# Modulation units of a two-layer diffusion trunk: fp32 weight-stationary matmuls on unsplit weights, at other places in the order

## The reference

```python
mod = silu(c) @ w_mod[layer] + b_mod[layer]   # 6 * 1024 columns, for c and for c_ctx
shift1, scale1, gate1, shift2, scale2, gate2 = split(mod, 6)
h = modulate(rmsnorm(x, g), shift1, scale1)   # h * (1 + scale) + shift
x = x + gate1 * rmsnorm(mixer(h), g)
h = modulate(rmsnorm(x, g), shift2, scale2)
x = x + gate2 * rmsnorm(ffn_or_moe(h), g)
```

## Time and profile before

| | us |
|---|---|
| three runs | 2237.32, 2241.19 (median), 2241.66 |
| span of the profiled execution | 2240.4 |
| PE busy in it | 2015.4 (90%) |
| DVE busy | 1433.3 (64%) |
| ACT busy | 1210.4 (54%) |
| data read from HBM | 471.27 MB, 211 GB/s |

### The profile page before, as it was taken

How to read it: one execution, slowest core, us unless ns; L and a number is a source line. 1 busy time by engine, 2 the same in 40 slices (tenths; PEclk the granted TensorE clock), 3 DMA queues, 4 the chain that set the end, 5 groups by cost and what they waited for, 6 DMA issues and landing times.

```text
span 2240.4 us, 25373 instructions
## 1 busy us (share of the span) xinstructions
PE 2015.4 (90%) x9386; PEld 1603.1 (72%) x9386; DVE 1433.3 (64%) x1355; ACT 1210.4 (54%) x1227; POOL 68.4 (3%) x124
## 2 busy tenths in 40 slices
PE   4699778699999977878979999999999999999996
PEld 3587546488887846853768878788787878878785
DVE  3545473633323336455458888888888888888885
ACT  3644353433322236433537767676777777776773
POOL 0011000000000000113000000000000000000000
PEclk9899889899999988986959999999999999999998
DMA  8455202143332214521028989899998989899891
GB/s 277 149 170 174 72 1 75 38 151 125 122 112 94 94 38 146 190 81 31 22 94 330 365 308 368 307 362 336 348 361 307 367 313 364 323 353 361 314 364 51
DMA packets 266582, 473.49 MB, mean 211 GB/s; under 512 B 19416, under 2 KB 119056, under 8 KB 266512
## 3 DMA queue, kind: packets, MB, share of 16 engines
q1 hardware_dynamic: 262928, 469.33, 59.5%
q0 software_dynamic: 3456, 3.19, 0.6%
q10 hardware_dynamic: 128, 0.03, 0.0%
HBM read 471.27 MB, written 1.05 MB: 211 GB/s over the span
## 4 chain that ended last, share of the span: by engine, by line
PE 79%; DVE 11%; ACT 5%; issue 3%; DMA 1%; ACTq 0%; SPq 0%; DVEq 0%; POOL 0%
PE bank L478 22%; PE bank L479 22%; PE bank L480 22%; PE bank L527 2%; PE bank L646 2%; DVE split_low L462 2%; ACT split_high L457 2%; PE bank L347 2%; DVE overlay L371 2%; PE bank L1657 2%; DVE split_low L1421 2%; ACT overlay L406 1%; PE bank L621 1%; PE bank L1699 1%; PE bank L636 1%
## 5 line engine op out<-in xcount | busy, mean ns | idle before, releaser
L1421 DVE TENSOR_TENSOR split_low<-raw_weights,split_high 128x2048 fp32r<-128x2048 f32 x224 | 511.7, 2287 | 59.8 <-ACT split_high L1115 58.8
L1115 ACT ACTIVATE split_high<-raw_weights 128x2048 fp32r<-128x2048 f32 x224 | 429.3, 1920 | 147.7 <-PE bank L480 147.7
L462 DVE TENSOR_TENSOR split_low<-raw_weights,split_high 128x1024 fp32r<-128x1024 f32 x214 | 256.9, 1224 | 372.2 <-ACT split_high L457 372.1
L478 PE MATMUL bank<-h_high,split_high 128*128 128x512 f32 (+1 forms) x848 | 329.3, 388 | 47.6 <-DVE h_low L392 30.5
L457 ACT ACTIVATE split_high<-raw_weights 128x1024 fp32r<-128x1024 f32 x214 | 219.5, 1051 | 227.9 <-PE bank L480 210.8
L479 PE MATMUL bank<-h_low,split_high 128*128 128x512 f32 (+1 forms) x848 | 322.8, 381 | 0.0
L480 PE MATMUL bank<-h_high,split_low 128*128 128x512 f32 (+1 forms) x848 | 322.7, 381 | 0.0
L1421 DVE TENSOR_TENSOR h_low<-raw_weights,h_high 128x2048 fp32r<-128x2048 f32 x112 | 256.7, 2292 | 78.7 <-ACT h_high L1115 78.6
L478 PE MATMUL bank<-split_high,xe_high 128*128 128x512 f32 x672 | 272.2, 405 | 14.0 <-DVE split_low L1421 14.0
L479 PE MATMUL bank<-split_low,xe_high 128*128 128x512 f32 x672 | 267.6, 398 | 0.0
L480 PE MATMUL bank<-split_high,xe_low 128*128 128x512 f32 x672 | 265.2, 395 | 0.0
(11 more groups left out here) (242 smaller groups left out, 3028.9 us busy)
## 6 DMA issues: line engine op xcount, KB each, us to landing
raw_weights<-in_moe_w SPq DMA_DIRECT2D x336, 1024.0 KB, 6.6
raw_weights<-in_w_mod SPq DMA_DIRECT2D x48, 1024.0 KB, 5.3
raw_weights<-in_ffn_w SPq DMA_DIRECT2D x33, 1024.0 KB, 5.2
raw_weights<-in_ev_w_in SPq DMA_DIRECT2D x10, 1024.0 KB, 5.8
raw_weights<-in_od_w_in SPq DMA_DIRECT2D x8, 1024.0 KB, 5.6
raw_weights<-in_ev_w_out SPq DMA_DIRECT2D x4, 1024.0 KB, 5.5
raw_weights<-in_od_w_out SPq DMA_DIRECT2D x4, 1024.0 KB, 5.3
overlay<-in_rpb SPq DMA_DIRECT2D x32, 64.0 KB, 2.3
```

The source lines that it names most:

```text
L462: dve.tensor_tensor(half_of(s, j, SPL[:, s % NSPLIT, :]), half_of(s, j, raw_of(split_at[s])), half_of(s, j, SPH[:, s % NSPLIT, :]).bitcast ...
L478: pe.matmul(ps, wh, xh, start=first, stop=False)
L1115: act.activation(esplit(u)[0], RAW[:, u % NRAW, :], ACT.Copy).then_inc(S("e_high"), 1)
L1421: dve.tensor_tensor(lo, RAW[:, u % NRAW, :], hi.bitcast(F32), ALU.subtract)\
```

## The change

A modulation unit is no longer split. `pe_mods` makes the raw weights stationary, 16 tiles of 128x128 in fp32, and streams the two vectors (two columns), so that the result lies across partitions at once; `dve_mods` adds the bias straight out of the bank. The halves of the vectors, the row copies, the small DMAs and the summing matmuls go. A unit's buffer is released by the matmuls and not by its split.

The units leave `ev`, `up` and `od`. Of the 48, numbers 0 to 7 stay in the start; 8 to 15 go into the first attention, two ahead of every second P.V product; 16 to 23 go between the heads' norm sums and `evo`; 24 to 27 behind n1's sums, 28 to 31 behind n2's; 32 to 35 behind n3's, 36 to 39 behind n4's; 40 to 43 behind ckv's sums, ahead of the latent products; 44 to 47 between n5's sums and n6's. The loads follow that order, and SP's bias loads for the second attention now stand ahead of those of units 44 to 47. The splits for `evo` and `odo` are no longer made ahead of the attentions: `to` is held at the last unit of `ev` and `od`.

```diff
@@ weight_units
-    units += mods(0, 0, 8)
-    for s in range(10):
-        units.append(("split", "ev", cols(w["ev_w_in"][0], 256 * s)))
-        units += mods(0, 8 + 2 * s, min(10 + 2 * s, 24))
-    units += [("split", "evo", cols(w["ev_w_out"][0], 256 * s)) for s in range(4)]
+    units += mods(0, 8)
+    units += [("split", "ev", cols(w["ev_w_in"][0], 256 * s)) for s in range(10)]
+    units += mods(8, 18)
+    for s in range(4):
+        units.append(("split", "evo", cols(w["ev_w_out"][0], 256 * s)))
+        if s == 1:
+            units += mods(18, 24)
+    units += mods(24, 28)
...
-        units += mods(1, s, min(s + 1, 8))
+        if s == 0:
+            units += mods(28, 32)
...
+    units += mods(32, 36)
...
-        units += mods(1, 8 + 2 * s, 10 + 2 * s)
+        if s == 1:
+            units += mods(36, 40)
+    units += mods(40, 44)
...
+    units += mods(44, 48)
@@ dve_modulate
             tmp(0)
             tmp(1)
+            if first:
+                first(0, 0)
@@ in place of pe_mod, act_mod, move_rows, pe_mod_third, dve_mod_third
+        def pe_mods(pe, i0, i1, bank, base=0):
+            for i in range(i0, i1):
+                r = mod_at[i]
+                pe.wait_ge(S(f"raw{r % NRAW}"), need[r])
+                wt = raw_of(r).rearrange("p (k n) -> p k n", k=KT)
+                c0 = base + 4 * (i % 24)
+                for m in range(2):
+                    for k in range(KT):
+                        last = pe.matmul(PS[bank][:, c0 + 2 * m:c0 + 2 * m + 2], wt[:, k, P * m:P * m + P],
+                                         SC[:, k, :], start=(k == 0), stop=(k == KT - 1))
+                last.then_inc(S("mod_used"), 1)
+
+        def dve_mods(dve, v0, v1, bank, base=0):
+
+            l, m0, c0, n = v0 // 6, 8 * (v0 % 6), base + 16 * (v0 % 6), v1 - v0
+            dve.wait_ge(S("mod_used"), 4 * v1)
+            dve.tensor_tensor(MOD[:, l, m0:m0 + 8 * n, :],
+                              PS[bank][:, c0:c0 + 16 * n].rearrange("p (m v) -> p m v", v=2),
...
+            dve.wait_ge(S("mod_evac"), v1)
@@ pe_attention
                     if p >= 2:
                         pe.wait_ge(S(f"o_evac{a}"), p - 1)
+                    if p % 2 == 0 and p // 2 < len(mods):
+                        pe_mods(pe, *mods[p // 2], OBANK[0], 256)
                     for kt in range(u["nk"]):
@@ SP
             for r in range(len(UNITS)):
+                if r == mod_at[44]:
+                    load_bias()
@@ ACT
-            to(0)
...
             act_root(act, N["n0"])
+            to(0, 0)
             act.wait_ge(S("affine"), 1)
...
             for g, s in run("ev"):
-                to(g + 1)
+                to(min(g + 1, of["ev"][-1]))
@@ DVE
+            to(of["evo"][1])
+            dve_mods(dve, 2, 6, 5, 256)
...
             to(of["evo"][-1] + 1)
@@ PE
-                pe_mod(pe, f)
+                pe_mods(pe, f, f + 1, 7)
...
-            pe_attention(pe, 0, att0)
+            pe_attention(pe, 0, att0, [(8 + 2 * p, 10 + 2 * p) for p in range(4)])
             for h in range(4):
                 pe_sums(pe, N[f"sub{h}"])
+            pe_mods(pe, 16, 24, 5, 256)
...
             pe_sum_pair(pe, N["n1"], 3)
+            pe_mods(pe, 24, 28, 7)
             pe.wait_ge(*norm_root("n1"))
             pe_sums(pe, N["n2"])
+            pe_mods(pe, 28, 32, 7)
...
             pe_sums(pe, N["n3"])
+            pe_mods(pe, 32, 36, 7)
             pe.wait_ge(*norm_root("n3"))
             pe_sums(pe, N["n4"])
+            pe_mods(pe, 36, 40, 7)
...
             pe_sums(pe, N["ckv"])
+            pe_mods(pe, 40, 44, 2)
             pe.wait_ge(*norm_root("ckv"))
...
             pe_sum_pair(pe, N["n5"], 3)
+            pe_mods(pe, 44, 48, 7)
             pe.wait_ge(*norm_root("n5"))
             pe_sums(pe, N["n6"])
```

More of the change, by code:

```diff
@@ L238, in trunk @@
                 of.setdefault(stage, []).append(ns)
-                full_after.append((full_after[-1] if ns else 0)
-                                  + (0 if stage == "down" else 1 if stage[:3] == "mod" else 2))
+                full_after.append((full_after[-1] if ns else 0) + (0 if stage == "down" else 2))
                 ns += 1
@@ L250, in trunk @@
                 release.append(("direct_used", nd))
-        stage_of = [UNITS[r][1] for r in split_at]
         def run(stage):
[L257 to L263, removed]
+            return [(s, i) for i, s in enumerate(of[stage])]
         token_major = [of["ev"][i] for i in (2, 3, 8, 9)] + [of["od"][i] for i in (4, 5)]
-        mod_index = {s: i for i, s in enumerate(of["mod0"] + of["mod1"])}
         def raw_of(r):
@@ L375, in mod_vectors, with dve_modulate @@
             return VEC[:, l, 2 * which], MOD[:, l, 24 * which:24 * which + 8]
-        def dve_modulate(dve, n, c0, full=False):
+        def dve_modulate(dve, n, c0, full=False, first=None):
             nt, wd = n["nt"], n["width"]
@@ L448, in half_free @@
                 return unit_used(old)
-            return bank_full(old, j) if stage_of[old][:3] != "mod" else unit_used(old)
+            return bank_full(old, j)
         def act_split(act, s, j):
@@ L515, in gemm_unit @@
             m.then_inc(S("bank_full"), 1)
[L517 to L564, removed]
@@ L613, in pair_out, with pe_attention @@
             return PS[OBANK[p % 2]][u["o"], :2 * P], (u["o"], t, slice(c, c + 2 * P))
-        def pe_attention(pe, a, units):
+        def pe_attention(pe, a, units, mods):
             def scores(i):
@@ L846, in experts, with load_bias @@
                     expert_load(b, NE - 1, u + NRAW)
+            def load_bias():
+                sp.wait_ge(S("n4_hl"), KT)
+                for i in range(NB_):
+                    h, qb = att1[i]["bias"]
+                    if i >= 2:
+                        sp.wait_ge(S("biased"), 2 * i - 2)
+                    for r in range(2):
+                        q_row = 2 * qb + r
+                        base = (h * (2 * ROWS - 1) + ROWS - 1 - q_row) * REPEAT * RPB_W + WIN_W - 1
+                        sp.dma_start(BT[64 * r:64 * r + 64, i % 2, :].rearrange("p (k n) -> p k n", k=4),
+                                     bass.AP(w["rpb"].tensor, base, [[RPB_W - 1, GRID], [REPEAT * RPB_W, ROWS], [1, GRID]]))\
+                          .then_inc(S(f"toeplitz{i % 2}"), 16)
             for r in range(len(UNITS)):
+                if r == mod_at[44]:
+                    load_bias()
                 if r >= NRAW:
@@ L853, in _ @@
                 load(r)
[L855 to L861, removed]
-                    base = (h * (2 * ROWS - 1) + ROWS - 1 - q_row) * REPEAT * RPB_W + WIN_W - 1
-                    sp.dma_start(BT[64 * r:64 * r + 64, i % 2, :].rearrange("p (k n) -> p k n", k=4),
-                                 bass.AP(w["rpb"].tensor, base, [[RPB_W - 1, GRID], [REPEAT * RPB_W, ROWS], [1, GRID]]))\
-                      .then_inc(S(f"toeplitz{i % 2}"), 16)
             experts(0)
@@ L888, in _ @@
             pool.dma_start(SBB, bass.AP(w["sgu_b"].tensor, 0, [[0, P], [1, 512]])).then_inc(S("sgu_b_in"), 16)
-            for n in range(4, 24):
-                move_rows(pool, n, f"mod_moved{n % 2}")
             for i in range(NB_):
@@ L1242, in _ @@
             dve_modulate(dve, N["n2"], 0)
+            dve_mods(dve, 6, 8, 7)
+            dve_affine(dve, 1, 0, 1.0, 8).then_inc(S("affine"), 1)
             for g, s in run("up"):
                 to(g + 1)
-                if s is not None and s % 2 == 1:
+                if s % 2 == 1:
                     p = s // 2
```

113 lines of the change are left out of this document (31 added, 82 removed).

## The result

| | before | after |
|---|---|---|
| median (lowest to highest), us | 2240.69 (2237.32 to 2241.66) | 2333.36 (2327.99 to 2334.44) |
| span of the profiled execution, us | 2240.4 | 2326.2 |
| mean granted clock in it | 0.947 | 0.904 |

The ratio is 1.0404, 95% interval 1.0386 to 1.0422: the changed kernel is 4% slower. The forecast was 2330 us.

A forecast was written before the change was run, and what follows sets the result against it. TensorE (PE) was taken as the bound, 79% of the chain; losses in the start, attention and norm blocks, less gains in ev, up and od, summed to +89 us, giving 2330 us, range 2255 to 2376.

The forecast's parts named there:

- start, to n0's reciprocal: Eight units before the first norm's reciprocal, all at clock 0.50, 6.8 us each: +25 us.
- attention 0: Four blocks of two units ahead of P.V products, DVE hiding about 3.2 us of each: +38, less 1 for beginning sooner.
- 16..24: Block of eight units ahead of evo, from 327.4 to 377.5 us, GEMM restarting at 0.50: +40 us.
- 40..44: Block of four units ahead of the latent products, 22.9 to 27.2 us, sums coming 6 us sooner: +15.5 us.
- 44..48: Four units between n5's and n6's sums: 25 us of units, 6.9 us of sums at 0.50: +21 us.
- The price and the clock: Per unit, PE pays 3.5 us at 2.4 GHz or 6.8 at 1.2, against 1.87 before; blocks fall to clock 0.50.
- The first 4.5 us or so at 1.00: A two-column block starts at full clock for 1.3 units, then runs at 0.50; two units take 9.3 us.
- the bound of -10: The start if its units ran at clock 1.00: it ends near 58.5 us, a shift of -10 us.
- The GEMMs: Units leaving the GEMM loops: ev -44.9 us, -53 with rope waits; up -15; od -38.8.
- The faster one: Rival: weight loads keep the clock at 1.00 everywhere, a unit is 3.5 us; 2179 us, chance 0.13.
- In between: Rival: blocks of two and four keep 1.00, the start and the block of eight don't; 2235 us, chance 0.10.
- Slower yet: Rival: every block at 0.50, attention 0 (+56) too, no re-rise in the sums; about +135, 2376 us, chance 0.12.

The follow-up runs named there:

- e3: The changed kernel with units 8 to 15 moved out of attention 0 to behind the heads' norm sums, one block of sixteen there: 2328.89 us.
- e6: 128 streamed columns in the new places, but attention 0 takes one unit ahead of each P.V product, not two ahead of every second: 2181.18 us.
- e1: The changed kernel with each unit matmul streaming 128 columns, the two vectors 64 times over, instead of two: 2182.18 us, ratio to before 0.9734.
- e7: 128 columns, new places, units spread thinner: ten at the start, eight singly in each attention, six ahead of evo: 2179.19 us, ratio to before 0.9718.

## Why the prediction was right, point by point

The shift of each step, measured by the same instructions in both traces (us; up ends where down begins, and down is in the row behind it):

| step | predicted | measured |
|---|---|---|
| start, to n0's reciprocal | +25 | +14.6 |
| to the end of ev's last GEMM | -51.5 | -51.9 |
| attention 0 | +37 | +52.4 |
| 16..24, to the end of evo's last GEMM | +40 | +41.6 |
| 24..28, to the end of n2's sums | +16 | +16.6 |
| 28..32 and up | -3 | -6.5 |
| 32..36, to the end of n4's sums | +16 | +14.0 |
| 36..40 and od | -29.8 | -33.4 |
| 40..44, to the first latent product | +15.5 | +17.9 |
| attention 1 | 0 | -0.9 |
| odo, to the end of n5's sums | +3 | +4.7 |
| 44..48, to the end of n6's sums | +21 | +20.5 |
| from there to the first expert's matmul | 0 | -0.8 |
| sum, to the first expert's matmul | +89 | +88.8 |

The first expert's matmul came at 1265.5 us ("near 1266"); the expert loops then took 3 us less, so the profiled span grew by 85.8 and the medians by 92.7.

- **The price and the clock** carried the sign, and both held. The 0.213 us of the earlier trace rows is what the blocks show at 0.50. "The first 4.5 us or so at 1.00" held in the block ahead of evo (predicted 50.1 us, measured 50.6) and in the two blocks ahead of a GEMM, up's and od's (22.9; measured 22.2 and 22.4). Those behind n1's and n3's sums kept 1.00 for some 2.5 us only (24.9 and 25.0), the one behind n5's for 2 (25.4, predicted 25), and the block ahead of the latent products had none of it, 27.3 us; that was the upper of the two values given. The 4.5 us were also read short from their own row: 0.74 over 396 to 399 us puts the fall at 397.4, 5.3 us after PE's last work. With 5.3 a block would have been priced some 0.7 us lower.
- **The start was mis-sized, by 10 us.** The step that failed is "nothing in the trace raised the clock on such a mix, so all at 0.50". Three of its eight units ran at the high clock (3.67, 3.52 and 3.78 us in the chain), 9.4 us less than 6.8 each. The norm sums behind them did not: 1.76 and 1.91 us, against 1.92 behind a low unit. The measured +14.6 lies between the value taken and the bound of -10.
- **Attention 0 was mis-sized, by 15 us, the other way.** Two assumptions of that step failed. The blocks didn't start at 1.00 and take 9.3 us; they took 13.65, 13.51, 11.79 and 13.66 us. Only the third had its start at 1.00; ahead of the first and the fourth the clock was low already, and the price of a block that starts high didn't hold there. And DVE hid nothing of them where 3.2 us each had been subtracted: without the blocks (e3) the stage is 57 us shorter, cutting them (e6) gained at most 2, and in e1, at the high clock, 28.3 of 32.3 us are paid with PE's idle time unchanged. In the kernel before DVE was 79% busy in this stage, which I read as cover. I now take it that PE and DVE work in turns there, each waiting for the other's last result, so that a block in PE's queue lengthens a turn by itself. Between its first two blocks the chain of e1 does go from PE to DVE and back twice (on DVE from 225.6 to 227.5 and from 230.9 to 233.8 us); that the turns are the reason is argued, and what is shown is the price and the idle time that stayed.
- These two misses nearly cancel, and that is luck: the total of +89 is better than its parts. Their size, 10 and 15 us, is what the working was good for.
- **The GEMMs** gave back what they were to give: ev's pairs and the rope waits 51.9 for 51.5, up and od, with the blocks ahead of them, 7 us more than predicted together. odo's first matmul waited as foreseen for its late split. One line of the timeline of the kernel after (start us, us, what, idle before):

```profile
1165.01 0.55 PE L473 MATMUL bank<-h_high,split_high 128*128 128x256 f32 x1 [4.28 <-DVE split_low L457]
```

- **The rivals.** The faster one needed the clock to stay; e1 made it stay and came to 2182 for its 2179. "In between" needed short blocks to keep 1.00: of those in attention, the shortest, one of four began at 1.00 and none kept it. "Slower yet" came nearest in attention 0 (+56 for +52.4) and had the rest too high.

Open: why the clock rose for three of the start's units, one behind another turn of the same kind that stayed low, why it fell with the second block in attention but only after some 4.5 us ahead of evo, and why it had fallen ahead of others. No run separates these, and none has a number of columns between two and 128. Not tried either: the split form of before in the new places.

## What to carry to other kernels

Before turning a product around so that the weights are stationary and few columns stream, price it by the records it makes (here two loads for each fp32 tile) and at the low clock, unless a row shows such a block at the high one; streaming surplus columns that nobody reads can be the cheaper way, and here it took the change from 4% slower to 2.7% faster. Put such work where PE stands waiting for a norm: there some 40 to 65% of it was free, more where its loads were in time (all but 3.5 of 21.6 us ahead of evo in e7), and it kept the next GEMM from starting low. In the attention loop it was paid in full, however it was cut, though PE had idle time there: by the reading above, idle time is cover only if the engine that PE waits for goes on working meanwhile.

## What the runs showed of the hardware

- A PE that is busy without a gap for 100 us with two-column fp32 matmuls stays at a granted clock of 0.50 (e3), and the same loads with 128 columns stay at 1.00 for the 21.5 us of a block (e1): 6.62 against 3.57 us a unit. PE and its loads were busy from end to end in both.
- The duration of a weight load goes with that clock. The source view of the unit matmuls, of after and of e1 (ns min/median/max, first and last start):

```profile
L520 PEld LDWEIGHTS bank<-silu_c,raw_weights x1536: 190/333/339, 20.7 to 1218.3; 128*128 128x128 f32 x192
```
```profile
L522 PEld LDWEIGHTS bank<-silu_c,raw_weights x1536: 186/192/339, 20.7 to 1076.8; 128*128 128x128 f32 x192
```

- Work of 64 times the columns cost 5% by itself: at 1.00 a record takes 0.112 us with 128 columns, and 0.107 in the first 4.5 us of a two-column block.
